# Normalising x between the stripes of the memory projection, and keys in four column tiles of 32

## The reference

```python
xn = rms_norm(x, norm_mix_g)                      # x * rsqrt(mean(x*x) + eps) * g
u_pool, q, k, v, logf, q_mem, gates = split_in(xn @ w_in, b_f)
mn = rms_norm(mem_prompt, mem_norm_g)             # 256 memory tokens
mk, mv = mn @ w_mem_k, mn @ w_mem_v               # 4 heads of 128 each
# attention of the sample group, for each sample: 8 heads, 8 queries, 1024 past keys + 8 new ones
s_past = jnp.einsum('bqhd,bkhd->bhqk', q, k_past) # k_past: 8 pages of 128 keys, by a page table
s_new = jnp.einsum('bqhd,bkhd->bhqk', q, k_new)
p = softmax(mask(concat([s_past, s_new]) * scale + bias))
o = p[..., :P] @ v_past + p[..., P:] @ v_new
```

## Time and profile before

| | |
|---|---|
| median of 3 runs | 4531.28 us (4523.84 to 4531.79) |
| profiled execution | 4530.24 us, its span 4528.6 us |
| granted clock of PE, mean | 0.965 |
| PE busy | 4260.5 us (94%) |
| DVE, ACT, POOL busy | 2641.4, 1249.2, 1632.8 us |
| HBM | 977.47 MB read, 81.33 MB written |

### The profile page before, as it was taken

The page is one execution under the profiler, slowest core; times in us unless marked ns, Lnnn a source line. Parts: engine busy times, 40 slices in busy tenths (PEclk is TensorE's granted clock), DMA queues, the critical chain, the costliest instruction groups (busy, mean ns, idle before and its releaser), DMA issues. The chain is left out here.

```text
span 4528.6 us, 76524 instructions
## 1 busy us (share of the span) xinstructions
PE 4260.5 (94%) x28688; PEld 4152.5 (92%) x28688; DVE 2641.4 (58%) x3611; ACT 1249.2 (28%) x1625; POOL 1632.8 (36%) x1257
## 2 busy tenths in 40 slices
PE   6999999999798899979999999998778999999997
PEld 5999999999665798979999999998778999999997
DVE  5222211111322453245878999996577898888887
ACT  4111233333212221132332233332122232323232
POOL 0000000000111000001457877787846676555652
PEclk8999999999788999989999999998899999999999
DMA  5722333333476443235778888887799999999996
GB/s 187 302 82 83 133 105 107 107 100 102 149 252 238 168 143 130 74 120 173 252 257 286 295 288 285 292 302 274 268 343 347 356 372 356 357 365 357 356 354 259
DMA packets 282479, 1061.61 MB, mean 234 GB/s; under 512 B 43762, under 2 KB 94322, under 8 KB 229170
## 3 DMA queue, kind: packets, MB, share of 16 engines
q1 hardware_dynamic: 165842, 524.29, 32.9%
q0 software_dynamic: 89888, 496.37, 29.9%
q10 hardware_dynamic: 26624, 39.37, 2.3%
HBM read 977.47 MB, written 81.33 MB: 234 GB/s over the span
## 5 line engine op out<-in xcount | busy, mean ns | idle before, releaser
L145 DVE TENSOR_TENSOR w_lo<-w_raw,w_hi 128x1024 fp32r<-128x1024 f32 x498 | 602.3, 1233 | 1019.6 <-ACT w_hi L136 1019.6
L136 ACT ACTIVATE w_hi<-w_raw 128x1024 fp32r<-128x1024 f32 x498 | 518.8, 1058 | 1184.3 <-PE acc L173 761.7
L1366 POOL DMA_INDIRECT routes_scratch<-gate_sums,route x384 | 582.0, 1516 | 143.6 <-issue 114.9
L173 PE MATMUL acc<-x_hi,w_hi 128*128 128x288 f32 x2592 | 557.0, 297 | 7.2 <-DVE w_lo L145 7.2
L173 PE MATMUL acc<-x_lo,w_hi 128*128 128x288 f32 x2592 | 556.6, 296 | 0.0
L173 PE MATMUL acc<-x_hi,w_lo 128*128 128x288 f32 x2592 | 556.4, 296 | 0.0
L173 PE MATMUL acc<-h_hi,w_hi_peeru 128*128 128x384 f32 (+1 forms) x1280 | 408.5, 335 | 42.4 <-DVE w_lo_peeru L145 42.4
L173 PE MATMUL acc<-h_hi,w_hi 128*128 128x384 f32 (+1 forms) x1280 | 404.0, 332 | 28.2 <-DVE w_lo L145 28.2
L173 PEld LDWEIGHTS acc<-x_hi,w_hi 128*128 128x128 f32 x2592 | 419.5, 189 | 7.6 <-DVE w_lo L145 7.6
L173 PEld LDWEIGHTS acc<-x_hi,w_lo 128*128 128x128 f32 x2592 | 419.3, 189 | 0.0
L173 PEld LDWEIGHTS acc<-x_lo,w_hi 128*128 128x128 f32 x2592 | 419.3, 189 | 0.0
(11 more groups left out here) (320 smaller groups left out, 8333.4 us busy)
## 6 DMA issues: line engine op xcount, KB each, us to landing
w_raw<-in_w_peer_u SPq DMA_DIRECT2D x256, 512.0 KB, 5.6
w_raw<-in_w_peer_v SPq DMA_DIRECT2D x256, 512.0 KB, 6.6
w_raw<-in_w_gate SPq DMA_DIRECT2D x96, 512.0 KB, 3.5
w_raw<-in_w_z SPq DMA_DIRECT2D x66, 512.0 KB, 3.3
k_ring<-in_cache_k SPq DMA_DIRECT2D x64, 512.0 KB, 4.9
v_ring<-in_cache_v POOLq DMA_DIRECT2D x64, 512.0 KB, 6.5
routes_scratch<-zero POOLq DMA_DIRECT2D x8, 3072.0 KB, 46.1
activations_scratch<-a_out ACTq DMA_DIRECT2D x128, 192.0 KB, 4.7
```

What stands on the lines that cost most here:

```text
L136: nc.scalar.activation(slot(q, j)[0], raw[:, j % 4, :], ACT.Copy).then_inc(q["hi"], 1)
L145: nc.vector.tensor_tensor(lo, raw[:, j % 4, :], hi.bitcast(F32), ALU.subtract).then_inc(q["lo"], 1)
L173: last = nc.tensor.matmul(dst, l_, r_[:, cc, c0:c0 + cn], start=(cc == first and p_ == 0), stop=(cc == last_c and p_ == 2))
L1366: pool.indirect_dma_start(route_dram, bass.IndirectOffsetOnAxis(ap=route[:, b, n:n + 1], axis=0), gsum[:, h % SUMS, b - 1, n % PTOP:n % PT ...
```

## The change

1. In stage 1, SP issues the load of the first block of mem_prompt ahead of g and the small constants, and after the weights also the first two blocks of x and the gain of its norm, which has a place of its own (`g_mix`).
2. Stages 2 to 4 become one block. ACT, DVE and PE run the norm of x between the eight stripes, in an order written out (below). High and low parts of the weights have four slots, x's blocks 2 to 4 are loaded by GpSimd, the recycle is gone, and the first halves of `w_z` are loaded at the end of this block.
3. In the attention, the 64 rows of a sample are two column tiles of 32: heads 0 to 3 and heads 4 to 7. A head's query block is 32 columns wide (`qz` has stride 40 in place of 72), the bias and mask matmuls are made for each tile, and heads alternate between the tiles, so that a pair of pages goes around four tiles.

```diff
@@ norm_transposed, SP
-                    if not got:
-                        sp.dma_start(g_row[:], ...).then_inc(s_g, 16)
+                    if load:
+                        sp.dma_start(x_of(0), load(0)).then_inc(s_x[0], 16)
+                    sp.dma_start(g_row[:], ...).then_inc(s_g, 16)
...
+                    if then_load:
+                        then_load(sp)
@@ the block of the memory projection
+                load_stripes(sp, a["w_mem"], NM, q)
+                load_first(sp, a["w_z"], q1, behind=q, halves=2 * NM)
+                sp.wait_ge(q["act"], 2 + NM)
+                sp.dma_start(a["mem_out"], mkv_t[:]).then_inc(s_mout, 16)
+                sp.wait_ge(s_mout, 16)
...
+            @block.gpsimd
+            def _(pool):
+                for b in range(2, NBLK):
+                    pool.wait_ge(s_xn, b - 1)
+                    pool.dma_start(xb[0:ROWS[b], b % 2, :], a["x"][b * P:b * P + ROWS[b], :]).then_inc(s_xl[b], 16)
...
+                def squares(b):
+                    n = ROWS[b]
+                    act.wait_ge(s_xl[b], 16)
+                    if b >= 2:
+                        act.wait_ge(s_tp, 4 * (b - 1))
+                    nc.scalar.activation(xn[0:n, b % 2, :], xb[0:n, b % 2, :], ACT.Square, accum_out=ss[0:n, b:b + 1]).then_inc(s_sq, 1)
...
+                split_hi(act, 0, 0, q)
+                for n in range(NM):
+                    if n < NBLK:
+                        squares(n)
+                    if n + 1 < NM:
+                        split_hi(act, (n + 1) // 2, (n + 1) % 2, q)
+                    if n < NBLK:
+                        root(n)
+                    if n >= 1:
+                        drain_mem(n - 1)
+                    if 2 <= n < NBLK + 2:
+                        hi_out(n - 2)
...
+                split_lo(dve, 0, 0, q)
+                dve.wait_ge(s_gx, 16)
+                for n in range(NM):
+                    if n < NBLK:
+                        mean(n)
+                    if n + 1 < NM:
+                        split_lo(dve, (n + 1) // 2, (n + 1) % 2, q)
+                    if n < NBLK:
+                        norm(n)
+                    if 2 <= n < NBLK + 2:
+                        lo_out(n - 2)
...
+                def turn(b):
+                    n = ROWS[b]
+                    pe.wait_ge(s_xn, b + 1)
+                    for g in range(4):
+                        if b >= 1:
+                            pe.wait_ge(s_xlo, 4 * (b - 1) + g + 1)
+                        for c in range(4):
+                            last = nc.tensor.transpose(tps[:, g, c * n:(c + 1) * n], ...)
+                        last.then_inc(s_tp, 1)
...
+                for n in range(NM):
+                    for h in range(2):
+                        pe.wait_ge(q["lo"], 2 * n + h + 1)
+                        if h == 0:
+                            pe.wait_ge(q["act"], n + 1)
+                        multiply_half(pe, n % 2, h, mn_hi, mn_lo, [(0, N_MEM)], q)
+                    if 1 <= n < NBLK + 1:
+                        turn(n - 1)
...
-        recycle(keep=[mix_got[0], *mix_got[1]])
-        norm_transposed("mix", NBLK, ROWS, ...)
@@ the attention
-        qz = then("qz", [P, 2, FOX * 72], F32)
+        qz = then("qz", [P, 2, FOX * 40], F32)
...
+                QUAD_HEADS = [4 * g + r for r in range(4) for g in range(2)]
+                def q_of(b, hh):
+                    c0 = 160 * (hh // 4) + 32 * (hh % 4)
+                    return qz[:, b, c0:c0 + 32]
...
-                            nc.tensor.matmul(s_logits[k // 4][b * 64:b * 64 + 64, :], negsel_s[:, 2 * u + b, :],
-                                             c_s[:, k * PAGE:(k + 4) * PAGE], start=True, stop=False)
+                            for g in range(2):
+                                r0 = b * 64 + 32 * g
+                                nc.tensor.matmul(s_logits[k // 4][r0:r0 + 32, :], negsel_s[:, 2 * u + b, 32 * g:32 * g + 32],
+                                                 c_s[:, k * PAGE:(k + 4) * PAGE], start=True, stop=False, tile_position=(0, r0))
...
-                    for hh in range(FOX):
+                    for hh in QUAD_HEADS:
                         for b, j in enumerate(slots):
-                            last = nc.tensor.matmul(s_logits[k // 4][b * 64:b * 64 + 64, (k % 4) * P:(k % 4 + 1) * P],
-                                                    qz[:, b, hh * 64:(hh + 1) * 64], k_ring[:, j % RING, hh * P:(hh + 1) * P],
+                            r0 = b * 64 + 32 * (hh // 4)
+                            last = nc.tensor.matmul(s_logits[k // 4][r0:r0 + 32, (k % 4) * P:(k % 4 + 1) * P],
+                                                    q_of(b, hh), k_ring[:, j % RING, hh * P:(hh + 1) * P],
```

More of the change, by code:

```diff
@@ L204, in multiply_stripes, with norm_transposed @@
                 between(pairs, (n - 1) % 2)
-        def norm_transposed(tag, n_blk, rows, g_in, x_of, load, x_hi, x_lo, stat, xn, beside=None, ahead=None, got=None):
+        def norm_transposed(tag, n_blk, rows, g_in, x_of, load, x_hi, x_lo, stat, xn, beside=None, ahead=None, then_load=None):
             ss_, ms_, r_ = stat
@@ L211, in norm_transposed @@
             s_tp, s_hi, s_lo = (sem(f"{tag}_{x}") for x in ("transposed", "hi_out", "lo_out"))
-            s_x = got[1] if got else [sem(f"{tag}_x_loaded{k}") for k in range(2)] if load else None
-            s_g = got[0] if got else s_g
+            s_x = [sem(f"{tag}_x_loaded{k}") for k in range(2)] if load else None
             with nc.Block() as block:
@@ L225, in _ @@
                     if load:
-                        for b in range(2 if got else 0, n_blk):
+                        for b in range(1, n_blk):
                             if b >= 2:
@@ new lines, in root, with hi_out @@
+                def root(b):
+                    n = ROWS[b]
+                    act.wait_ge(s_ms, b + 1)
+                    nc.scalar.activation(ms[0:n, b:b + 1], ms[0:n, b:b + 1], ACT.Sqrt).then_inc(s_rt, 1)
+                def hi_out(b):
+                    n = ROWS[b]
+                    for g in range(4):
+                        act.wait_ge(s_tp, 4 * b + g + 1)
+                        nc.scalar.activation(x_hi[:, 4 * g:4 * g + 4, b * P:b * P + n], tps[:, g, 0:4 * n].rearrange("p (c t) -> p c t", c=4),
+                                             ACT.Copy).then_inc(s_xh, 1)
@@ L333, in _, with mean, norm, lo_out @@
             def _(dve):
-                with dve.Fori(0, MEM) as i:
-                    split_lo(dve, i, 0, q)
-                    split_lo(dve, i, 1, q)
+                def mean(b):
+                    n = ROWS[b]
+                    dve.wait_ge(s_sq, b + 1)
+                    nc.vector.tensor_scalar(ms[0:n, b:b + 1], ss[0:n, b:b + 1], 1.0 / D, EPS, ALU.mult, ALU.add).then_inc(s_ms, 1)
+                def norm(b):
+                    n = ROWS[b]
+                    dve.wait_ge(s_rt, b + 1)
+                    nc.vector.reciprocal(rstd[0:n, b:b + 1], ms[0:n, b:b + 1]).then_inc(s_r, 1)
+                    dve.wait_ge(s_r, b + 1)
+                    nc.vector.scalar_tensor_tensor(out=xn[0:n, b % 2, :], in0=xb[0:n, b % 2, :], scalar=rstd[0:n, b:b + 1],
+                                                   in1=g_mix[0:n, :], op0=ALU.mult, op1=ALU.mult).then_inc(s_xn, 1)
+                def lo_out(b):
+                    n = ROWS[b]
+                    for g in range(4):
+                        dve.wait_ge(s_xh, 4 * b + g + 1)
+                        nc.vector.tensor_tensor(x_lo[:, 4 * g:4 * g + 4, b * P:b * P + n], tps[:, g, 0:4 * n].rearrange("p (c t) -> p c t", c=4),
+                                                x_hi[:, 4 * g:4 * g + 4, b * P:b * P + n].bitcast(F32), ALU.subtract).then_inc(s_xlo, 1)
+                split_lo(dve, 0, 0, q)
[9 more added lines that the diff above has]
+                        lo_out(n - 2)
                 for m in range(2):
@@ L342, in _ @@
             def _(pe):
-                multiply_stripes(pe, 2 * MEM, mn_hi, mn_lo, [(0, N_MEM)], q, use=("act",))
-                pe.wait_ge(q["act"], 2 + 2 * MEM)
+                def turn(b):
+                    n = ROWS[b]
+                    pe.wait_ge(s_xn, b + 1)
+                    for g in range(4):
+                        if b >= 1:
+                            pe.wait_ge(s_xlo, 4 * (b - 1) + g + 1)
+                        for c in range(4):
+                            last = nc.tensor.transpose(tps[:, g, c * n:(c + 1) * n], xn[0:n, b % 2, (4 * g + c) * P:(4 * g + c + 1) * P],
+                                                       ident[0:n, 0:n])
+                        last.then_inc(s_tp, 1)
+                pe.sem_inc(q["mm"], q["slots"])
+                pe.sem_inc(q["act"], 2)
+                for n in range(NM):
[6 more added lines that the diff above has]
+                        turn(n - 1)
+                pe.wait_ge(q["act"], 2 + NM)
                 for m in range(2):
+                    pe.wait_ge(s_xlo, 4 * NBLK)
```

70 lines of the change are left out of this document (40 added, 30 removed).

## The result

| | before | changed |
|---|---|---|
| median of the comparison (4 runs each) | 4529.7 us | 4486.1 us (4481.4 to 4492.2) |
| ratio, 95% interval | | 0.9904 (0.9891 to 0.9917) |
| profiled execution, its span | 4530.2, 4528.6 us | 4489.1, 4487.4 us |
| mean granted clock | 0.965 | 0.967 |

Two later timings of the same kernel gave 4496.8 and 4488.9 us (ratios 0.9926, 0.9908 to 0.9945, and 0.9924, 0.9898 to 0.9951). All 16 executions have a mean of 4492.3 us, the 26 of the kernel before beside them 4529.5: 37.2 us. So part of the 43.6 is the luck of one set, and some 8 us are a real error.

What follows compares the result with a forecast made beforehand. It took an engine chain to bound the norm of x and PE's own instructions mostly the attention. Terms 10.0 + 0 + 7.2 + 7.6 + 4.8 = 29.6 us off 4530.2 gave 4500.6, median 4502 us; range 4488 to 4518.

Steps and rivals of the forecast that it cites:

- edit 1: Norm of x moved between the memory projection's stripes: first split of w_z at 99.1 instead of 109.16, 10.0 us gained.
- unit 0: First attention phase, keys without values: faster pairs offset by three late-clock steps (6.6 us) and late keys, about 0 gained.
- unit 1: Second attention phase, keys with values: eight steps shrink from 5.25 to 4.36 us, 7.2 us gained.
- unit 2: Third attention phase, steps of 6 us and more: faster key pairs gain 7.6 us.
- unit 3: Fourth attention phase, already waiting for keys: 4.8 us taken of a possible 7.6.
- the loop: Norm of x between stripes: the hand-ordered chain between ACT, DVE and PE sets the pace, 11.5 us per block.
- Rival 1: Attention, unit 0: the clock rises as early as before, 6.6 us more gain, 4495 us; chance 0.28.
- Rival 2: Attention, unit 0: clock stays at half until values join in step 10; unit loses 10 us, total 4512; chance 0.2.
- Rival 3: Attention: DMA is the bound, steps with values shrink only to 5.15 us, total 4514; chance 0.08.
- Rival 4: Attention: key pairs get no faster because weights set their pace; edit 1 alone, 4521 us; chance 0.03.
- rival 6: Attention key pairs: column tiles run one after another, 3.5 us a pair, 51 us lost, 4572 us; chance 0.01.
- Rival 5: Attention, unit 1: the clock does not come back there either, 22 us lost, about 4541 us; chance 0.05.

Runs made afterwards that it cites:

- quarter_keys: The changed kernel loading only the first quarter of every key page of units 1 to 3, which leaves some logits wrong; 4484.3 us, ratio 0.9906.
- after_again: The changed kernel itself, unmodified, timed a second time; 4496.8 us, ratio 0.9926.
- heads_in_order: The changed kernel with a key pair's heads in order 0 to 7, so two column tiles are in use at a time; 4504.0 us, ratio 0.9941.
- norm_only: The changed kernel with the attention of before, so only the norm of x between the stripes is new; 4515.6 us, ratio 0.9972.
- after_third: The changed kernel itself, unmodified, timed a third time; 4488.9 us, ratio 0.9924.
- pair1_late: The changed kernel with unit 0's second key pair issued in step 2 instead of step 1; 4491.0 us, ratio 0.9915.
- pair2_early: The changed kernel with unit 0's third key pair issued in step 1, behind the second; 4487.7 us, ratio 0.9905; a second execution, marked _b, took 4476.4 us.

## Why the prediction was wrong

Terms of the sum, in us gained: as forecast, in the profiled execution of the changed kernel, and as the mean over its three profiles.

| term | forecast | profiled | three profiles |
|---|---|---|---|
| edit 1, to the first split of w_z | 10.0 | 10.2 | 11.0 |
| unit 0 | 0 | 8.2 | 6.0 |
| unit 1 | 7.2 | 8.3 | 7.9 |
| unit 2 | 7.6 | 10.3 | 9.3 |
| unit 3 | 4.8 | 2.4 | 3.7 |
| sum | 29.6 | 39.4 | 37.9 |

- **Edit 1** was right in place, mechanism and size: the loop, its releaser, the stalls of about 3 us and the store behind it. Of its 2.0 us at the start the profiled execution had only 0.3 (first split of w_mem at 23.35, 23.68 before); in the fifteen other executions with this start it came between 21.3 and 23.1, nine times by 21.8, the 2 us of the forecast. Over the thirteen executions with this loop the first split of w_z starts between 96.9 and 101.6, on average at 99.3.
- **Unit 0, the step that failed.** "I forecast three steps" of late clock, -6.6 us. The mechanism is real and its price was right (4.68 against 2.60 us a step). The number of late steps was wrong: in the profiled execution none, over eight executions none to two, and unit 0 gives 3.7 to 8.2 us, on average 5.9, instead of 0. Rival 1, at 0.28, was what happened in the one execution of the timed set that has a trace. The forecast took one case of a quantity that varies between executions as if it were fixed, and took one step later than the latest seen. The 1.0 us that it took off for late keys was too much as well: the steps are 2.60 us, and only the last pair waits, 0.2 to 0.6 us in the three profiles. Rival 2, half clock until step 10, is out: the latest rise of all executions is 24.1 us after the first logits, within unit 0.
- **Units 1 and 2** were right in mechanism, and too small by the price of a pair. A step saved 5.25 - 4.22 = 1.03 us, not 0.89: a four-tile run directly ahead of another shows none of its tail (0.90 us). The half-clock step at the head of a unit gave more than 0.89 too: from 7.4 to 5.8 us in unit 1 and from 8.3 to 6.0 in unit 2 (5.1 to 6.7 and 6.0 to 7.3 over the three profiles).
- **Unit 3** was right in mechanism: DMA takes back what PE saves, and quarter_keys shows it. Both sizes were too small, and nearly cancel: without the DMA's load the unit gives 67.1 - 55.9 = 11.2 us, where 7.6 were taken for PE, and the DMA takes back 6 to 9, where 2.8 were. Rival 3, DMA as the bound of all of unit 1, is out: there the step is 4.22 us. But the rings do run out at its end. In after_again its last steps take 5.09 and 5.11 us, near the 5.15 of the forecast, with PE waiting for keys; in quarter_keys they take 4.65.

```profile
1257.64 1.08 PE L1046 MATMUL acc<-k_ring,qz 128*32 128x128 f32 x32 [0.18 <-DMA k_ring<-in_cache_k]
...
1262.75 1.08 PE L1046 MATMUL acc<-k_ring,qz 128*32 128x128 f32 x32 [0.19 <-DMA k_ring<-in_cache_k]
```

- **Rival 4** (no faster pair) and **rival 6** (weight loads one after another) are out by 1.05 us for 32 records; but heads_in_order shows that the pair is set by two things, its columns and the tiles in turn, where the forecast knew one. Rival 5 needed a clock that stays at half through unit 1; there only the first pair ran at half clock, in every kernel.
- **The median.** The remaining 6 us between the mean gain (37.2) and that of the first set (43.6) are spread between executions, and that the first median fell below the range by 2 us is luck on top of the error in unit 0. The two later medians lie inside the stated range.

## What to carry to other kernels

Read a queue written out by hand as a loop, and add what stands in each engine's queue between a release and the next: that gave a loop of 11.5 us here, where 11.07 and 11.80 were measured. It also names the cure, which is to issue what another engine waits for (the low parts) ahead of what it doesn't; that was worth 13 us more. A clock that comes back after a stall is to be forecast as a spread over executions, not as a number of steps; one profile, and even two, give the wrong idea of it. Where PE is quickened next to loads, look per stage at whether the DMA share is already near 1.

## What was not expected of the hardware

At a granted clock of 1.00 the same matmuls run at two paces. Busy time by stretch, the z projection: first norm_only, then the changed kernel's third profile in two stretches (all 128x288, in the same order).

```profile
150.00:450.00 300.00, 300.00 (x2310) 300.00 (x2309) 68.16 (x73) 58.09 (x72) 0.00 (x0) 1.00 0.34 119
```

```profile
150.00:450.00 300.00, 300.00 (x2252) 300.00 (x2252) 65.27 (x71) 56.98 (x71) 0.00 (x0) 1.00 0.33 116
600.00:1000.00 400.00, 400.00 (x3079) 400.00 (x3078) 78.82 (x65) 128.24 (x129) 0.00 (x0) 1.00 0.33 107
```

2310 in 300 us are 130 ns each, 2252 are 133; 3079 in 400 us are 130 again. The pace also changes within an execution: norm_only has 3002 in 600:1000, which is 133 again. In norm_only this saved 10 us from the first split of w_z to the attention (1071.8 us; 1081.5 to 1083.5 where the pace did not change), in after_third 17. Neither the kernel nor the granted clock explains it. It is most of why norm_only's profile lies 13 us more below the kernel before than edit 1 gives. Single executions of one kernel differ by 10 to 37 us (4505.8 to 4543.0 for the kernel before in one call), and this pace is one part of that. Another lies in the expert layer, between the attention and the last norm, which no edit touches: it took 2399.4 us in pair1_late and 2420.9 in pair2_early, with 2308 and 2314 us of busy PE, so mostly more waiting. Of the 30.1 us between pair2_early and pair2_early_b, 10.2 lie ahead of the attention and 19.5 in the expert layer (2401.4 us in pair2_early_b). The size of a change of 0.2% can't be read from one span; it can from the starts of its own stage.
